# The last round of a mixture of experts: last up weights in two transfers over all experts, closing sums ordered by column piece, layer-norm statistics by 256 columns

## What is computed

```python
def hierarchical_moe(x, w_router_group, w_router_expert, w_gate, w_up, w_down):
    ...
    h = (jax.nn.silu(jnp.einsum('td,edf->tef', xt, w_gate))
         * jnp.einsum('td,edf->tef', xt, w_up)
         * combine[..., None].astype(x.dtype))
    return jnp.einsum('tef,efd->td', h, w_down).reshape(nb_, s_, d_)

def reference(...):
    ...
    ffn = hierarchical_moe(x, ...)
    x = layer_norm(alpha * x + ffn, ln2_g[l], ln2_b[l])   # over 1024 channels
```

## Time and profile before

| | |
|---|---|
| time, median of 3 runs | 391.96 us (391.88 to 392.21) |
| profiled execution, own time | 392.52 us |
| its span | 390.3 us |
| PE busy | 359.8 us, 92% |
| DVE busy | 161.5 us, 41% |
| ACT busy | 137.5 us, 35% |
| DMA moved | 132.79 MB, mean 340 GB/s |
| chain that ended last | PE 67%, DMA 17%, SP's queue 8%, DVE 5% |

### The profile page before, as it was taken

One profiled execution on the slowest core, in us unless ns is written; L12 is line 12 of the kernel. 1 busy time (PEld: TensorE's weight loads), 2 busy tenths in 40 slices (PEclk: granted clock), 3 DMA queues, 4 the chain that ended last, 5 costly groups with the idle time before them and its releaser, 6 DMA issues.

```text
span 390.3 us, 8014 instructions
## 1 busy us (share of the span) xinstructions
PE 359.8 (92%) x3331; PEld 283.8 (73%) x3331; DVE 161.5 (41%) x338; ACT 137.5 (35%) x239; POOL 35.0 (9%) x42
## 2 busy tenths in 40 slices
PE   5999999999999999999899999999499599299986
PEld 5899989999999999998666666666255356157632
DVE  3556479797464767464730303030510110110226
ACT  4653565555535344434722222222111212112012
POOL 7000000000000000001000004307710000000001
PEclk9999999999999999999999999999789889799999
DMA  8699884966759659699999999999999999999972
GB/s 277 195 331 385 283 282 154 368 224 217 251 174 343 244 179 319 187 402 411 408 384 423 425 426 426 425 425 424 427 424 413 422 425 427 427 425 424 415 282 108
DMA packets 52581, 132.79 MB, mean 340 GB/s; under 512 B 2834, under 2 KB 36642, under 8 KB 41540
## 3 DMA queue, kind: packets, MB, share of 16 engines
q1 hardware_dynamic: 52100, 131.88, 87.1%
q0 software_dynamic: 304, 0.17, 0.2%
q10 hardware_dynamic: 144, 0.26, 0.2%
HBM read 131.25 MB, written 1.05 MB: 339 GB/s over the span
## 4 chain that ended last, share of the span: by engine, by line
PE 67%; DMA 17%; SPq 8%; DVE 5%; ACT 2%; issue 1%; DVEq 0%; ACTq 0%
PE bank L1177 15%; DMA gu<-in_w_up 14%; PE bank L1471 11%; PE bank L1206 10%; PE bank L1339 6%; PE bank L1506 6%; PE bank L1209 5%; PE bank L1422 4%; PE bank L1518 4%; SPq L416 3%; SPq L447 3%; PE bank L1321 3%; DMA raw<-in_w_in 3%; PE bank L1276 1%; DVE wl L811 1%
## 5 line engine op out<-in xcount | busy, mean ns | idle before, releaser
L811 DVE TENSOR_TENSOR wl<-raw,wh 128x1024 fp32r<-128x1024 f32 x54 | 65.9, 1224 | 55.0 <-ACT wh L629 54.9
L1471 PE MATMUL bank<-gu,xg 128*32 128x256 f32 x1024 | 64.5, 414 | 17.5 <-DMA gu<-in_w_up 16.9
L629 ACT ACTIVATE wh<-raw 128x1024 fp32r<-128x1024 f32 x54 | 56.6, 1056 | 59.6 <-PE bank L1177 20.4
L1471 PEld LDWEIGHTS bank<-gu,xg 128*32 128x32 f32 x1024 | 34.3, 119 | 44.4 <-issue 25.3
L1206 PE MATMUL bank<-xh,wh 128*128 128x256 f32 x176 | 44.1, 288 | 0.9 <-ACT qT L691 0.9
L1206 PE MATMUL bank<-xl,wh 128*128 128x256 f32 x176 | 43.1, 283 | 0.0
L1206 PEld LDWEIGHTS bank<-xh,wh 128*128 128x128 f32 x176 | 33.6, 191 | 3.1 <-issue 2.0
L1075 DVE TENSOR_SCALAR xg<-bank,gcol,bcol 128x128 f32<-128x128 f32 x32 | 10.9, 404 | 59.0 <-PE bank L1422 59.0
L1206 PEld LDWEIGHTS bank<-xl,wh 128*128 128x128 f32 x176 | 33.7, 191 | 0.0
L1422 PEld LDWEIGHTS bank<-pick,x1p 128*128 128x128 f32 x256 | 29.8, 192 | 1.9 <-issue 0.9
L1422 PE MATMUL bank<-pick,x1p 128*128 128x128 f32 x256 | 30.2, 276 | 0.6 <-DVE pick L1046 0.6
(11 more groups left out here) (235 smaller groups left out, 584.6 us busy)
## 6 DMA issues: line engine op xcount, KB each, us to landing
gu<-in_w_gate SPq DMA_DIRECT2D x32, 1024.0 KB, 14.0
gu<-in_w_up SPq DMA_DIRECT2D x31, 1024.0 KB, 19.6
dn<-in_w_down SPq DMA_DIRECT2D x26, 1024.0 KB, 17.1
raw<-in_w_in SPq DMA_DIRECT2D x40, 512.0 KB, 4.8
raw<-in_w_o SPq DMA_DIRECT2D x8, 512.0 KB, 4.8
raw<-in_w_out_conv SPq DMA_DIRECT2D x4, 512.0 KB, 3.3
raw<-in_w_out_attn SPq DMA_DIRECT2D x4, 512.0 KB, 4.9
x<-in_x SPq DMA_DIRECT2D x2, 512.0 KB, 3.9
```

What stands on the lines that cost most here:

```text
L629: act.activation(wh[:, s, :].rearrange("p (k c) -> p k c", k=KC), raw[:, pair % NRAW, :].rearrange("p (k c) -> p k c", k=KC) [:, :, n % 2 ...
L811: dve.tensor_tensor(wl[:, s, :].rearrange("p (k c) -> p k c", k=KC), raw[:, pair % NRAW, :].rearrange("p (k c) -> p k c", k=KC) [:, :, n % ...
L1471: mm = pe.matmul(bank[6 - part][g, 0:DE], xg[:, k, g], w[:, e, part, k, :], start=(k == 0), stop=(k == KC - 1), skip_group_check=True)
```

## The change

Three things change, and one threshold with them.

The gates of the last quad are issued as before (`load_last_gates`). Its up matrices now come in two transfers over all four experts (`load_last_ups`, `UP_PARTS`): chunks 0 to 5 (3 MB) and chunks 6 and 7 (1 MB). PE issues six `stay_warm` matmuls ahead of its wait for the first, does 24 matmuls, waits for the second, and does 8.

In the last round the scatter of piece 1 is done for both tiles, then that of piece 2 for both, and each of the latter waits for a new semaphore, `third_read`: DVE must have read the sums of columns 512:768 of that tile first.

The statistics are taken by 256 columns, four for each tile (`statistics(t, piece)`), and `scaled` is computed ahead of those of piece 1.

POOL begins `x1n` at NY * bounds[3] in place of 2 * bounds[4].

```diff
-WARM_LAST = 2, 4, 6
+WARM_LAST = 6, 0
+UP_PARTS = ((0, KC - 2), (KC - 2, KC))
...
-            def load_last_gu(c):
+            def load_last_gates():
 
                 for e in range(QE):
-                    for i in range(2 if c and e == QE - 1 else 1):
-                        ks = slice(i * KHALF, (i + 1) * KHALF) if c and e == QE - 1 else slice(0, KC)
-                        sp.dma_start(gu[(NQ - 1) % 2][:, e, c, ks, :],
-                                     (wg_v, wu_v)[c][:, (NQ - 1) * QE + e, ks, :]
-                                     ).then_inc(last_up_end if i else last_gu_in[c][e], 16)
+                    sp.dma_start(gu[(NQ - 1) % 2][:, e, 0, :, :],
+                                 wg_v[:, (NQ - 1) * QE + e, :, :]).then_inc(last_gate_in[e], 16)
+
+            def load_last_ups():
+
+                for i, (lo, hi) in enumerate(UP_PARTS):
+                    sp.dma_start(gu[(NQ - 1) % 2][:, :, 1, lo:hi, :],
+                                 wu_v[:, (NQ - 1) * QE:NQ * QE, lo:hi, :]).then_inc(last_up_in[i], 16)
...
-            pool.wait_ge(y_ps, 2 * pool.value_load(bounds[0:1, 4:5], min_val=1, max_val=MAX_ROUNDS))
+            pool.wait_ge(y_ps, NY * pool.value_load(bounds[0:1, 3:4], min_val=1, max_val=MAX_ROUNDS))
...
                 take_y(c)
+                dve.engine_nop().then_inc(third_read, TT)
                 take_gathered(c + 2)
...
-            dve.wait_ge(added, first + 1)
-            dve.bn_stats(stats[:, 0, 0, :], bank[0][:, :])
+            def statistics(t, piece):
+
+                at = piece * SEQ
+                return dve.bn_stats(stats[:, t, piece, :], bank[2 * t + at // HALF][:, at % HALF:at % HALF + SEQ])
+
+            for t in range(TT):
+                dve.wait_ge(added, first + t + 1)
+                for piece in range(2):
+                    statistics(t, piece)
             take_y(last)
-            dve.wait_ge(added, first + TT)
-            dve.bn_stats(stats[:, 1, 0, :], bank[2][:, :])
             dve.tensor_tensor(scaled, bank[0][:, :], lng[:, 0:HALF], ALU.mult).then_inc(scaled_done, 1)
             for t in range(TT):
-                dve.wait_ge(added, first + TT + (NY - 1) * (t + 1))
-                link(dve.bn_stats(stats[:, t, 1, :], bank[2 * t + 1][:, :]))
-                variance(t)
+                dve.wait_ge(added, first + TT + t + 1)
+                statistics(t, 2).then_inc(third_read, 1)
+            for t in range(TT):
+                dve.wait_ge(added, first + 2 * TT + t + 1)
+                link(statistics(t, 3))
+                variance(t, 4)
...
-                            if last_quad:
+                            if last_quad and part == 0:
                                 for e in range(QE):
-                                    pe.wait_ge(last_gu_in[part][e], 16)
-                                    if part and e < QE - 1:
-                                        stay_warm(WARM_LAST[e])
+                                    pe.wait_ge(last_gate_in[e], 16)
                             for k in range(KC):
-                                if last_quad and part == 1 and k == KHALF:
-                                    pe.wait_ge(last_up_end, 16)
+                                if last_quad and part == 1:
+                                    for i, (lo, _) in enumerate(UP_PARTS):
+                                        if k == lo:
+                                            stay_warm(WARM_LAST[i])
+                                            pe.wait_ge(last_up_in[i], 16)
...
+                            scatter(1)
                             for t in range(TT):
-                                scatter(1, [t])
+                                pe.wait_ge(third_read, TT * c + t + 1)
                                 scatter(2, [t])
```

More of the change, by code:

```diff
@@ L115, in hybrid_block @@
         half_neg = sb("half_neg", [P, TT])
-        stats = sb("stats", [P, TT, 2, 6])
+        stats = sb("stats", [P, TT, 4, 6])
         moments = sb("moments", [P, TT, 2])
@@ L274, in hybrid_block @@
         dn_left_in = [sem(f"dn_left_in{j}") for j in range(FC)]
-        last_up_end = sem("last_up_end")
-        last_gu_in = [[sem(f"last_gu_in{c}{e}") for e in range(QE)] for c in range(2)]
+        last_gate_in = [sem(f"last_gate_in{e}") for e in range(QE)]
+        last_up_in = [sem(f"last_up_in{i}") for i in range(len(UP_PARTS))]
         out_done = sem("out_done")
@@ L340, in hybrid_block @@
         y_taken = [sem(f"y_taken{i}") for i in range(NY)]
+        third_read = sem("third_read")
         pick_done = sem("pick_done")
@@ L531, in _ @@
             sp.wait_ge(gu_ps, through(NQ - 2))
-            for c in range(2):
-                load_last_gu(c)
+            load_last_gates()
+            load_last_ups()
             sp.wait_ge(y_ps, NY * through(NQ - 1))
@@ L951, in _, with variance @@
                 y_low(JP - 1, m)
-            def variance(t):
-                link(dve.bn_aggr(moments[:, t, :], stats[:, t, :, :]))
+            def variance(t, parts):
+                link(dve.bn_aggr(moments[:, t, :], stats[:, t, 0:parts, :]))
                 dve.tensor_scalar(moments[:, t, 1:2], moments[:, t, 1:2], EPS, None,
@@ L966, in _ @@
                 link(dve.bn_stats(stats[:, t, 1, :], x1[:, t, HALF:DM]))
-                variance(t)
+                variance(t, 2)
             dve.wait_ge(x1T_ps, 4)
```

## The result

The changed kernel takes 397.44 us, median of 6 runs (395.83 to 399.24); the kernel before, on the same chip, 392.08 (391.60 to 393.48). The ratio is 1.0117, with a 95% interval of 1.0092 to 1.0142. Forecast were 392.25, at most 392.9: the change costs about 4.6 us (0.0117 x 392), where +0.3 was expected. The ratio on record is not the quotient of the two medians, which is 1.0137, or 5.4 us; the text goes by ratios, since they come with an interval. The profiled execution took 399.24, the longest of the six, and the kernel before 392.52 in its own.

The account below looks back on a forecast made before the run. In the last 25 us the weight stream and PE were taken to bound the kernel together, arriving almost at once. Part 1's +0.05, inside part 2's +0.28 for `centre`, gave +0.3 on the median 391.96: 392.25 us, range 391.5 to 392.9.

Parts of the forecast that it names:

- the first term of part 1: Last quad's up matrices: the first transfer, 3 MB, lands 3 x 2.46 us after the last gate's 359.1, at 366.5.
- part 1: Last quad's up matrices in two transfers: stream +0.2 us, PE's 1.5 us gain lost waiting for down weights; +0.05 in all.
- Part 2: Last scatters and 256-column statistics: tile 0 read 0.55 us later, `centre` starts 0.28 later, last store taken as +0.3.
- The sum: Whole kernel: the parts together cost +0.3 us, giving a median of 392.25.
- The part on POOL and the nop: Earlier start of `x1n` on POOL and each round's nop on DVE: no cost, with 20 us of slack for `x1n`.
- Rival 6: End of the last round: PE's clock falls to half after the new 1.5 us wait, up to +5 us (397); chance 0.03.
- Rivals 3: Last round: part 1's 1.5 us reach the end because the stream too runs earlier; 390.7 us; chance 0.04.
- Rival 5: Last round: slower rows make the stream 0.7 us or more late, last down product holds scatter; +0.8, 392.8; chance 0.07.

Follow-up runs that it names:

- e1: Kernel before with only `stats` declared twice as large, so every tensor behind it starts 96 bytes later; 396.28 us, ratio 1.0084.
- e9: Kernel before with only 128 unused bytes ahead of `stats`, so the weight buffers start 128 past a multiple of 256; 396.17 us, ratio 1.0097.
- e4: Kernel before with only the change's scatters and statistics, `gu0` at byte 27520, not a multiple of 256; 396.86 us, ratio 1.0098.
- e6: Kernel before with only the change's scatters and statistics, weight buffers where they were before; 392.77 us, ratio 1.0003.
- e12: Changed kernel at its own addresses, with ten spare matmuls in place of six ahead of the up product and four behind `down(0, [0])`; 396.52 us, ratio 1.0107.
- e3: Kernel before with only the change's up matrices, `gu0` at 27392 as before; 393.19 us, ratio 1.0000.
- e8: e5 with four spare matmuls behind `down(0, [0])`, in PE's wait for `dn_left_in[1]`; 393.96 us, ratio 1.0025.
- e10: e3 run once more, the kernel before with only the change's up matrices; 392.66 us, ratio 1.0020.
- e11: e5 run once more, with more rounds; 392.64 us, ratio 1.0008.
- e5: Whole changed kernel with `stats` moved behind all other tensors, so weight buffers start at multiples of 256 as before; 393.59 us, ratio 1.0009.
- e7: Kernel before with 96 unused bytes ahead of `gu1`, while `gu0` and `dn` stay at multiples of 256; 394.12 us, ratio 1.0034.
- e2: Changed kernel with 32 more bytes ahead of `stats`, so `gu0` starts at 27520, a multiple of 128; 397.28 us, ratio 1.0109.

## Why the prediction was wrong

**What failed** is the first term of part 1, "The first transfer is 3 MB and lands at 359.1 + 3 x 2.46", and with it the sum: the stream's landings of before were carried over unchanged, and only edited transfers were priced. The larger declaration of `stats` had no term at all, though it stands in the full kernels. It is the one edit that touches every transfer of weights. Its price: 0.84 to 0.97% for the kernel before with nothing but the shift (e1, e9), 0.95% for the scatters and statistics (e4 less e6), 1.1% for the whole change (1.0117 against 1.0009 and 1.0008). So 3.3 to 4.3 us of the 4.6 come from where the buffers lie, each difference uncertain by about 1 us. The upper end may hold part of the clock's fall too, since later landings make PE's waits longer. Between 202 us and the last gate some 65 transfers of 1 MB follow each other; at 0.042 each that is 2.7 of the 3.0 us. The step is the measure to trust here, and not one landing: the last gate lands between 358.1 and 360.5 in seven traces at multiples of 256, and between 360.1 (e12) and 362.8 in six off them.

**Part 1, +0.05.** The stream's cost was about right where the buffers lie as before, its effect was not. In e3's trace the 3 MB land at 366.47 and the 1 MB at 369.02 (forecast 366.5 and 369.1), PE's second half of the first down product starts at 374.24 (374.34), behind a wait of 1.27 (1.5), and the ratio is 1.0000. From the last gate to the last piece it takes 20.24 us before, and 0.1 to 0.3 more in e3, e8, e10 and e11, where +0.2 was forecast between 0.1 and 0.7; in e5 it is 1.2 more, outside that range. The forecast let only 0.05 of its 0.2 through, on the ground that the scatter waits for the copy of piece 1 and not for the last landing. The traces say otherwise: `centre` starts 4.16 to 4.17 behind the last landing in the four traces with the old scatters in which that comes late (before, e1, e9, e10), while its distance from the copy varies between 3.94 and 4.22. Only where the copy comes over 0.3 behind the last landing (e3, e7) does it hold `centre`, 3.88 behind it. In the kernel before, the last landing holds `centre`, by 0.06 us over the copy, so a later last landing passes on in full. In the changed kernel's trace the 3 MB took 7.93 us in place of 7.37.

**Part 2, +0.28 for `centre` and +0.55 for tile 0.** Right to 0.1 us. In e6, counted from the copy of piece 1, `centre` comes 0.32 later than before and POOL's power for tile 0 0.53 later, but this sets a trace held by the copy against one held by the last landing. Like with like: where the last landing holds `centre`, it follows 4.38 to 4.39 behind with the new scatters (e4, e5, e11, e12) and 4.16 to 4.17 without, +0.22, and POOL's power 3.58 to 3.59 and 3.14 to 3.15, +0.44; where the copy holds it, 4.25 to 4.26 (changed, e2, e6, e8) and 3.88 (e3, e7), +0.37. In e5 the last piece lands at 379.65, and DVE shows:

```profile
379.63 0.42 DVE L1121 COPY ys<-bank 128x256 f32<-128x256 f32 x1 [0.70 <-PE bank L1523]
...
384.04 1.54 DVE L1163 SCALAR_TENSOR_TENSOR gu<-bank,moments,lng 128x512 f32<-128x512 f32 x2
```

Statistics of 256 columns take 0.43, as taken. What was not priced is that the aggregation of four parts takes 0.27, against 0.21 of two.

**The sum, +0.3.** For the edited instructions alone the two measurements give +0.3 us (0.0008 and 0.0009 x 392), with intervals from -0.5 to +1.2. The forecast's size and sign fit, but the intervals hold no change too, and the differences of the medians, 0.85 (e5) and 0.33 (e11), are as far apart.

**The part on POOL and the nop.** No run shows a cost. `x1n` starts at 262.60 in place of 265.51, but it does so anywhere from 262.8 to 267.2 in the eight traces with the old threshold, so the new one can't be seen to do anything.

**Rival 6, the clock, 0.03.** Given too little. It did happen in the changed kernel's trace and in two others (e2, e3), for 3.4 us each, at a price of 1.3 to 1.6 us for `scatter(0)` and 1.4 to 1.5 up to `centre`, not the 5 that stood in the forecast as its most. The argument against it was a stretch in which PE was busy for 1.23 of 3.00 us at full clock; what was not asked is whether PE's waits in the last round would be as harmless there. The prediction also set against it, by the Trainium skill, TensorE: Matmul & The Clock Gate, section Why this matters for your kernels, that a longer gap is needed. The traces don't agree: the clock fell behind waits of at most 1.59 us.

**Rivals 3 and 5.** The stream did not run earlier, against 3: in e3 the last piece lands at 379.43, 0.10 later than before. Rival 5 has the right mechanism, the last pieces late, by the wrong cause and a sixth of the size: they were 4.1 late, 3.0 of it before the edited transfers.

What is open: the cost of the fall on the median. All three profiled executions that had it are among the longest of their kernel (the longest of 6, the longest of 5, the second longest of 12), so other executions may have gone without; but e11's, the longest of its 12, had none. Open too is the first up transfer, 3 MB in rows of 6 KB, which took 7.36 to 8.50 us in five traces at multiples of 256 and 7.53 to 7.93 in three off them, so that no order by address is seen.

## What to carry to other kernels

When a diff changes the shape of any on-chip tensor, work out the start address of every tensor declared behind it, and compare it modulo 256 with before; in a kernel bound by its weight stream, as this one, it can outweigh all that the edit is for. A stream that is slower in a stretch where nothing was edited is the sign of it, so compare GB/s of an unedited window first. Small tensors whose size may change belong behind the large buffers, or get a gap that keeps the sum at a multiple of 256.

## What the runs showed of the hardware

**The start of the rows in SBUF sets the stream's rate.** Rows of 8 KB from HBM into buffers at multiples of 256: 2.445 to 2.454 us per MB in seven traces, 424 or 425 GB/s over 230 to 350. At 96 or 128 past such a multiple: 2.486 to 2.489 in six traces, 420 or 421. 128 is no better than 96; other distances were not tried. The three transfers of 1 MB in rows of 2 KB (`dn` of the last quad) took 2.57 us each before (368.92 to 376.64), and 2.66 in e1 (372.61 to 380.59), +3.4%; over all traces they took 2.54 to 2.57 in the seven and 2.64 to 2.69 in the six, +4% by the means. The second up transfer, also in rows of 2 KB, took 2.48 to 2.59 in five and 2.70 to 2.71 in three, +7%.

The Trainium skill, DMA: Bandwidth & Descriptors, section How a descriptor splits into AXI transactions, says that a descriptor is cut into transactions of 256 B and that one which doesn't start at a multiple of 256 B begins at the boundary below, which adds a transaction. By it, as an estimate if time went by transactions, a row of 8 KB has 33 in place of 32 (+3.1%) and one of 2 KB 9 in place of 8 (+12.5%). The same section says that the bytes ahead of the start still cost beats, of 32 B each: by beats, again an estimate, it is +1.2% to +1.6% for 8 KB and +4.7% to +6.3% for 2 KB, the first number at 96 past and the second at 128. The traces agree that 128 is not enough and 256 is, and that short rows suffer more. The measured sizes, +1.7% and +3.4% to +7%, lie near the estimate by beats and far from that by transactions, though no difference between 96 and 128 is seen. The page puts it as a matter of what is read, and here it is the side written to that moved.

**The clock can fall after short waits.** PE's idle time ahead of the up product and ahead of the second half of the first down product, and the clock in the 4 us behind, in the eight traces with the new up transfers:

| kernel | first wait | second wait | clock falls to half |
|---|---|---|---|
| changed | 1.59 | 1.53 | yes, 3.4 us |
| e2 | 0.84 | 1.56 | yes, 3.4 us |
| e3 | 0.67 | 1.27 | yes, 3.4 us |
| e11 | 0.56 | 1.17 | no |
| e5 | 0.76 | 1.14 | no |
| e12 | about 0.1 | 0.42 | no |
| e10 | none | 0.34 | no |
| e8 | none | none | no |

The second wait orders the eight; the first doesn't (0.67 with a fall, 0.76 without), so that it plays a part isn't shown. In e12 spare matmuls filled waits that would have been about 1.0 and 1.5 us by its landings, as long as in e2, and there was no fall. Eight traces are no rule, and a fall of this length can be missed in the times: e3 had one in its profiled execution, and a ratio of 1.0000.
